# Around the last RWKV norm: output products dealt out, residual rows unscaled and loaded sooner, four up blocks among the last transposes

## What is computed

```python
rw_out, new_wkv = rwkv7_group(p_shift, ...)        # ends in: yn = (y - mu) * rsqrt(var + GN_EPS) per head
out = (yn * gn_g + gn_b + bonus) * g               # the end of rwkv7_group
mix = jnp.concatenate([rw_out, att_out], axis=-1) @ w_out
x = layer_norm(DEEPNORM_ALPHA * x + mix, ln1_g, ln1_b)
up = x @ ffn_w_up
u_conv, u_lin = up[..., :D_FF], up[..., D_FF:]     # D_FF = 2816
h = jax.nn.silu(conv(u_conv)) * u_lin
x = layer_norm(DEEPNORM_ALPHA * x + h @ ffn_w_down, ln2_g, ln2_b)
```

## Time and profile before

| | us |
|---|---|
| median of 3 runs | 1758.98 (1752.64 to 1760.13) |
| profiled execution | 1760.66 |
| its span, first to last instruction | 1758.6 |
| TensorE busy | 1618.3 (92%) |
| VectorE busy | 921.3 (52%) |
| ScalarE busy | 684.9 (39%) |
| GpSimd busy | 336.0 (19%) |
| mean granted clock of TensorE | 0.947 of 2.4 GHz |

### The profile page before, as it was taken

One profiled execution on the slowest core, in us unless ns is written; L12 is line 12 of the kernel. 1 busy time (PEld: TensorE's weight loads), 2 busy tenths in 40 slices (PEclk: granted clock), 3 DMA queues, 4 the chain that ended last, 5 costly groups with the idle time before them and its releaser, 6 DMA issues.

```text
span 1758.6 us, 39976 instructions
## 1 busy us (share of the span) xinstructions
PE 1618.3 (92%) x17211; PEld 1167.1 (66%) x17211; DVE 921.3 (52%) x2144; ACT 684.9 (39%) x1162; POOL 336.0 (19%) x209
## 2 busy tenths in 40 slices
PE   6989999998999778988767979999999999999998
PEld 4457666664667566666646856666666666888887
DVE  3579999985768557767431762333322222100046
ACT  5633233114677546665533233333333333411110
POOL 2431111002211101221112011111111222121100
PEclk9789999998999789988878989999999999999999
DMA  5232122235622112100114221111111111421002
GB/s 217 72 116 98 49 70 78 76 103 169 184 54 59 29 45 80 40 22 3 51 35 150 85 88 49 48 48 49 49 48 49 48 48 49 176 73 49 25 16 85
DMA packets 50113, 126.69 MB, mean 72 GB/s; under 512 B 17266, under 2 KB 24082, under 8 KB 42098
## 3 DMA queue, kind: packets, MB, share of 16 engines
q1 hardware_dynamic: 48850, 123.08, 20.7%
q0 software_dynamic: 1088, 1.05, 0.2%
HBM read 100.34 MB, written 23.77 MB: 71 GB/s over the span
## 4 chain that ended last, share of the span: by engine, by line
PE 82%; DVE 7%; ACT 5%; issue 3%; DMA 1%; SPq 1%; DVEq 0%; ACTq 0%
PE bank L2272 79%; PE bank L2429 1%; PE bank L1013 1%; PE bank L958 1%; DVE arena L2022 1%; DMA arena<-x 1%; DVE arena L2065 1%; ACT L1394 1%; ACT arena L2476 0%; DVE arena L2035 0%; SPq L765 0%; DVE arena L1636 0%; DVE arena L2018 0%; SPq L769 0%; DVE arena L2019 0%
## 5 line engine op out<-in xcount | busy, mean ns | idle before, releaser
L2272 PE MATMUL bank<-arena 64*64 64x64 f32 (+10 forms) x16504 | 1533.6, 289 | 121.8 <-issue 22.1
L2272 PEld LDWEIGHTS bank<-arena 128*128 128x128 f16 (+6 forms) x16504 | 1089.8, 124 | 564.2 <-issue 140.0
L2783 POOL TENSOR_TENSOR arena<-arena 128x2048 f16<-128x2048 f32 x53 | 215.8, 4073 | 826.5 <-ACT arena L2476 826.5
L2671 DVE TENSOR_SCALAR_CACHE_REDUCE arena<-arena 128x384 bf16<-128x384 f32 (+6 forms) x231 | 196.9, 918 | 1.2
L2475 ACT ACTIVATE arena<-arena 128x2048 f16<-128x2048 f32 x53 | 100.8, 1902 | 158.0 <-PE bank L2272 139.3
L2076 DVE TENSOR_SCALAR arena<-arena 128x1072 f32<-128x1072 f32 x22 | 18.9, 859 | 186.7 <-issue 173.8
L2492 ACT ACTIVATE arena<-bank 128x352 f32<-128x352 f32 x72 | 33.4, 464 | 192.6 <-PE bank L2272 192.6
L1770 POOL TENSOR_TENSOR arena<-arena 128x512 f32<-128x512 f32 x40 | 54.4, 1368 | 259.5 <-PE bank L2272 127.0
L2476 ACT ACTIVATE arena<-arena 128x2048 f32<-128x2048 f32 x53 | 100.6, 1898 | 0.0
L2088 DVE SCALAR_TENSOR_TENSOR arena<-bank,arena 128x352 f32<-128x352 f32 (+1 forms) x66 | 33.9, 514 | 120.4 <-PE bank L2272 93.5
L2003 ACT ACTIVATE arena<-arena 128x1056 f16<-128x1056 f32 x22 | 23.9, 1085 | 131.0 <-DVE arena L2090 131.0
(11 more groups left out here) (269 smaller groups left out, 1176.1 us busy)
## 6 DMA issues: line engine op xcount, KB each, us to landing
arena<-slabs SPq DMA_DIRECT2D x53, 1024.0 KB, 4.9
arena<-kcache SPq DMA_DIRECT2D x32, 256.0 KB, 2.9
arena<-vcache SPq DMA_DIRECT2D x32, 256.0 KB, 3.0
prw<-arena SPq DMA_DIRECT2D x42, 176.0 KB, 1.9
arena<-xt SPq DMA_DIRECT2D x4, 1056.0 KB, 10.2
x1d<-arena SPq DMA_DIRECT2D x8, 512.0 KB, 2.6
arena<-x1d SPq DMA_DIRECT2D x1, 4096.0 KB, 13.0
y<-arena SPq DMA_DIRECT2D x8, 512.0 KB, 2.6
```

Of the source, the lines that this page charges most:

```text
L2272: return nc.tensor.matmul(out, lhsT, rhs, start=start, stop=stop, skip_group_check=True)
L2671: last = dve.tensor_scalar(junk, a, s, None, op, ALU.add, accum_out=cnt[:, k:k + 1])
L2783: pool.tensor_tensor(WL[r].rearrange("p a b -> p (a b)"), STG[s], WH[r].rearrange("p a b -> p (a b)"), ALU.subtract).then_inc(slab_lo, 1)
```

## The change

- `out` is dealt: token tile 0 after `ch` 7, tile 1 after `cen`, tile 2 after `var`, tiles 3 and 4 after `zg` of the last period. All five now belong to item 7.
- The last item's `YS, SQ, YC, RSTD, FO` move to another place in `arena` (`NORM`), which frees the place of residual rows 5 to 8 once `y` of item 7 is read. SP waits for that, loads these rows ahead of slab 17, then slab 17, the norm's parameters and slab 18. Its wait for the last `wkv_p` stores stands before slab 19.
- No residual row is scaled by ALPHA, here and before the second norm: products are added with UN / ALPHA, and LN_EPS is divided by ALPHA squared. `resid_scaled` is gone. VectorE waits for the first five rows before the first residual, for the others after the first sampled part.
- GpSimd's split of slab 16 waits until `y` of item 7 is read.
- Four up blocks (f = 0 and 1, m = 0; n = 0 and 1) are made inside `ln1_order`: n = 0 after "t1" 6, n = 1 after "t1" 7. Their ScalarE copies stand at the same places.

```diff
 RW_PERIOD = (
...
+    ("fin", "a", 1), ("ch", "c", 2), ("bo", "a"), ("lp", "b", 4), ("zg", "d"), ("out", "d", 3), ("out", "d", 4), ("fin", "a", 2), ("fo", "d", 2), ("scale", "p", 0), ("ch", "c", 3),
...
+    ("zgate", "z0"), ("bv", "a"), ("y", "c"), ("split", "s", 0), ("ch", "c", 7), ("out", "c", 0), ("lp", "a", 1), ("ss", "p"), ("zscan", "z0"), ("cen", "c"), ("out", "c", 1),
+    ("gh", "b"), ("scan", "p"), ("lx", "a", 1), ("zsquare", "z0"), ("var", "c"), ("out", "c", 2), ("km", "p"), ("zkm", "z0"), ("ry", "b"), ("lp", "a", 2),
...
-            if not 0 <= items[who] < NI or (kind == "out" and k < NI + 2) or (kind == "fin" and k == 1):
+            if not 0 <= items[who] < NI or (kind == "out" and items[who] != NI - 1) or (kind == "fin" and k == 1):
...
         if t >= 2:
             steps.append(("t1", t - 2))
+        if t == TQ:
+            steps += [("up", (0, 0)), ("up", (1, 0))]
+        if t == TQ + 1:
+            steps += [("up", (0, 1)), ("up", (1, 1))]
     return steps
...
+        NORM = [(YS, SQ, YC, RSTD, FO)] * (NI - 1) + [tuple(words(XT0 + HT * n, HT) for n in range(5))]
...
-            def out(i):
-                out_halves(SL_OUT, range(4, KT), range(OUT_EARLY))
+            def out(_, t):
+                out_halves(SL_OUT, range(4, KT), (t,))
...
-            def ch(i, n):
-
-                if i == NI - 2 and n < X1E:
-                    if n == 0:
-                        act.wait_ge(resid_in, 16)
-                    act.activation(X1[:, n, :], X1[:, n, :], ACT.Copy, scale=ALPHA)
-
...
             def wsplit(n):
+                if n == 1:
+                    emptied(pool, ("y", NI - 1))
                 split(SL_OUT + n)
...
         def late_sync(sp, load_slab):
-            sp.wait_ge(mx_ready, 1)
+            emptied(sp, ("y", NI - 1))
+            sp.dma_start(X1[:, X1E:TQ, :], i["x"][P * X1E:T].rearrange("(t p) n -> p t n", p=P)).then_inc(resid_in, 16)
+            sp.dma_start(X1[0:NS, TQ, :], i["x"][T:TOK]).then_inc(resid_in, 16)
             load_slab(SL_OUT + 2)
+            sp.dma_start(LN1P.rearrange("p a b -> p (a b)"), i["ln1"].broadcast_to([P, 2 * DM])).then_inc(ln1_in, 16)
             load_slab(SL_OUT + 3)
-            for t in range(X1E, TQ):
-                sp.dma_start(X1[:, t, :], i["x"][P * t:P * t + P]).then_inc(resid_in, 16)
-            sp.dma_start(X1[0:NS, TQ, :], i["x"][T:TOK]).then_inc(resid_in, 16)
-            sp.dma_start(LN1P.rearrange("p a b -> p (a b)"), i["ln1"].broadcast_to([P, 2 * DM])).then_inc(ln1_in, 16)
+            sp.wait_ge(wkv_out, 16 * HP)
...
+                if kind == "up":
+                    emptied(pe, ("t1", (2, 5)[t[1]], 1))
+                    cols(SL_UP + t[0], (0,), (t[1],))
+                    continue
...
         def late_scalar(act, link, split):
 
-            act.wait_ge(resid_in, 16 * (1 + TQ - X1E + 1))
-            split(SL_OUT + 2)
-            act.activation(X1[:, X1E:TQ, :], X1[:, X1E:TQ, :], ACT.Copy, scale=ALPHA)
-            act.activation(X1[0:NS, TQ, :], X1[0:NS, TQ, :], ACT.Copy, scale=ALPHA).then_inc(resid_scaled, 1)
-            for w in (SL_OUT + 3, SL_UP, SL_UP + 1):
+            for w in (SL_OUT + 2, SL_OUT + 3, SL_UP, SL_UP + 1):
                 split(w)
...
-            act.wait_ge(resid_in, 16 * (TQ - X1E + 4))
-            act.activation(Y2, Y2, ACT.Copy, scale=ALPHA)
-            act.activation(Y2S[0:NS], Y2S[0:NS], ACT.Copy, scale=ALPHA).then_inc(resid_scaled, 1)
...
         def late_vector(dve, link):
-            dve.wait_ge(resid_scaled, 1)
-            dve.wait_ge(ln1_in, 16)
+            dve.wait_ge(resid_in, 16)
...
                 part(n)
+                dve.wait_ge(resid_in, 16 * 3)
                 for t in (first, TQ, *range(first + 1, TQ)):
                     residual(n, t)
+            dve.wait_ge(ln1_in, 16)
```

More of the change, by code:

```diff
@@ L337, in late_banks @@
             continue
+        if kind == "up":
+            b.add(("col", SL_UP + t[0], 0, t[1]), "act")
+            continue
         for w in (SL_OUT + 2, SL_OUT + 3):
@@ L341, in late_banks @@
     for f in range(FT):
-        cols(SL_UP + f, by=("act", "dve"))
+        if f < UP_EARLY:
+            b.add(("col", SL_UP + f, 0, 2), "act")
+            cols(SL_UP + f, (1,), by=("act", "dve"))
+        else:
+            cols(SL_UP + f, by=("act", "dve"))
     for n in range(4):
@@ L1109, in cen @@
                 emptied(pe, ("y", i))
-                channel_sums("cen", i, CEN, YS)
+                channel_sums("cen", i, CEN, NORM[i][0])
             def var(i):
                 emptied(pe, ("cen", i))
-                channel_sums("var", i, ONES2, SQ)
+                channel_sums("var", i, ONES2, NORM[i][1])
             def zg(i):
                 low_rank(i, "zg")
-            def out(i):
-                out_halves(SL_OUT, range(4, KT), range(OUT_EARLY))
+            def out(_, t):
+                out_halves(SL_OUT, range(4, KT), (t,))
             rows_of = lambda h4: slice(NS * h4, NS * h4 + NS)
@@ L1399, in fo @@
                 emptied(act, ("zg", i))
-                act.activation(MXH[0][:, i // 2, HT * (i % 2):HT * (i % 2) + HT], FO, ACT.Copy, scale=XS).then_inc(fo_hi, 1)
+                act.activation(MXH[0][:, i // 2, HT * (i % 2):HT * (i % 2) + HT], NORM[i][4], ACT.Copy, scale=XS).then_inc(fo_hi, 1)
             def zgate(_):
@@ L1476, in rw_scalar @@
             steps = {"lmix": lmix, "ltanh": ltanh, "scale": scale, "gate": gate, "square": square, "scan": scan, "ln": ln, "norm": norm, "tl": tl, "am": am, "bv": bv,
-                     "lp": level_products, "wz": wz, "ry": ry, "ch": ch, "cen": cen, "var": var, "rstd": rstd, "fo": fo,
+                     "lp": level_products, "wz": wz, "ry": ry, "cen": cen, "var": var, "rstd": rstd, "fo": fo,
                      "zgate": zgate, "zscan": zscan, "zln": zln, "znorm": znorm, "split": wsplit, "ztl": ztl, "za2": za2, "zwt": zwt,
@@ L1898, in late_tensor @@
             for f in range(FT):
-                cols(SL_UP + f)
+                if f < UP_EARLY:
+                    cols(SL_UP + f, (0,), (2,))
+                    cols(SL_UP + f, (1,))
+                else:
+                    cols(SL_UP + f)
             last_g = len(DN_G) - 1
@@ L1986, in late_scalar @@
                 u = UPB[:, f % 2, :]
-                for n in range(3):
+                for n in range(2 if f < UP_EARLY else 0, 3):
                     b = wait_job(act, ("col", w, 0, n))
@@ L2294, in three, with cols @@
                 return last
-            def cols(w, ms=(0, 1)):
+            def cols(w, ms=(0, 1), ns=range(3)):
                 pe.wait_ge(slab_lo, w + 1)
@@ L2300, in cols @@
                 for m in ms:
-                    for n in range(3):
+                    for n in ns:
                         b = open_bank(pe, ("col", w, m, n))
```

35 lines of the change are left out of this document (22 added, 13 removed), and 3 rows, old and new, of the table RW_PERIOD.

## The result

| | before | changed |
|---|---|---|
| median, us | 1758.05 (1752.64 to 1760.13, 4 runs) | 1716.61 (1713.03 to 1721.34, 4 runs) |
| ratio | | 0.9768 (0.9749 to 0.9787) |
| span of the profiled execution | 1758.6 | 1713.0 |
| mean granted clock | 0.947 | 0.963 |

The kernel is 41.4 us faster by the medians; 33.8 were forecast, with a range that ended 1.4 us above what came. The question is where 8 us more came from (12 by the two profiled spans).

What follows compares the result with a forecast made beforehand. TensorE's own work was taken as 82% of the path, so gains must come where it idles or is slow. Terms 1.6 + 3.4 + 5.3 + 10.1 + 4.3 + 9.1 = 33.8 us gave 1725.2 us, range 1718 to 1739.

Steps and rivals of the forecast that it cites:

- Part 1: Between products of RWKV items 6 and 7: ScalarE no longer scales five residual rows; gain 1.6 us, bounds 0 to 2.85.
- Sum 1.6 us: Same place: TensorE's waits behind the scaling ACTIVATEs, some 1.0 us and 0.6 us, taken as the whole gain.
- Part 2: Item 7's state steps: moving GpSimd's slab 16 split shortens item 6's mxl; gain 3.4 us, bounds 0 to 3.4.
- Part 3: Last item's norm: five output tiles dealt over it, y's end to mx_ready 18.4 to 13.1; gain 5.3 us, bounds 2.7 to 7.4.
- Parts 4 and 5: Output stage: unscaled, earlier-loaded residual rows remove TensorE's hole, 10.1 us; low clock after two pauses goes, 4.3 us.
- rival C: Output stage: a new wait for a slab or rows, 5 us and half the clock; about 1732 us; chance 0.09.
- Part 6: Last transposes before up projection: four up blocks fill TensorE's holes, 7.6 us, plus clock 1.5; gain 9.1, bounds 5 to 9.4.
- the 1.7 us gap stays: After the last transpose: TensorE's 1.73 us wait for the last evacuation was to remain despite the up blocks.
- A: Last item's norm: clock stays low, 2.7 us gained instead of 5.3, output stage begins at 0.50; 1730.5 us; chance 0.17.
- B: RWKV items 6 and 7: parts 1 and 2 hidden by another wait; 5.0 us less, 1730.2 us; chance 0.10.
- D: Last transposes: the up blocks fill nothing; 9.1 us less gain, 1734.3 us; chance 0.06.
- E: Up or down projection: lower clock for d us costs d/2; chance 0.04 for d over 85, 0.04 for 50 to 85.

Runs made afterwards that it cites:

- u_split: Changed kernel without GpSimd's wait for y of item 7 ahead of slab 16's split; y 6 to y 7 took 22.1 us, no whole time given.
- u_deal: Changed kernel with all five output tiles again between ch 7 and cen of the last item; 1728.26 us, ratio 0.9831 to the kernel before.
- again_after: Changed kernel, unchanged, profiled once more; 875.3 us from y of item 5 to the end.
- u_rescale: Changed kernel with only ScalarE's scaling of residual rows back; mx_ready to the first transpose 54.2 us, no whole time given.
- u_load: Changed kernel with only the late row loads back, after mx_ready and two slabs; mx_ready to the first transpose 54.2 us, no whole time given.
- The longer row: Changed kernel, unchanged, timed again with five rounds; median 1720.35 us, ratio 0.9767 to the kernel before.

## Why the prediction was right or wrong

**Part 1** was mis-sized most for its size: 1.6 forecast, 3.4 came in the first pair (31.7 - 28.3), and 3.8 between the means of the four executions with the ACTIVATEs (31.4) and the eleven without (27.6). Its direct half was right, 0.63 + 1.03 us of waits; the step that failed is "Sum 1.6 us", and with it the high bound of 2.85, which left out the lower clock of the 68 products behind the waits (4.66 us for 3.01).

**Part 2**: 3.4 forecast, 3.45 came in the first pair (22.13 - 18.68), and u_split gives the cause. That is the upper end: with the split in its new place the stage has two lengths, 18.7 and 19.6, and the means of nine such executions and of the four with the old place are 2.7 apart.

**Part 3**: 5.3 forecast; 18.4 to 11.6 is 6.8, but at the same rise of the clock it is 5.2 (u_deal). The forecast's chain put the rise 3.9 us after y's end, as before. It came after 0.6. In again_after it came after 3.9, and there `cen` was read at 4.35 for the 4.3 of the forecast, Ln ended at 7.4 for 7.4, and mx came at 13.2 for 13.1. So the working was right, and the 1.5 more is luck; the means of the four executions with the tiles in one piece and the nine with them dealt out, 17.4 and 12.2, give 5.2 too.

**Parts 4 and 5**: 10.1 + 4.3 = 14.4 forecast, 68.7 - 54.2 = 14.6 came. The clock was 1.00 in the whole stage. What the text missed is that either half of the edit does it alone: it gave the gain to the loads and to the scaling together, and rival C (a new wait of 5 us) reckoned a late slab or row at a price, though VectorE's adds can start 7 us after mx, or stop for 5.5, at no cost, as u_rescale and u_load show.

**Part 6**: 9.1 forecast, 10.8 came (771.7 - 760.9), 11.5 and 12.1 by other pairs. The filled holes are the 7.6 of the forecast. The step that failed is "the 1.7 us gap stays": it shrank to 0.77. VectorE's evacuations for the last transposes, before and changed:

```profile
1030.66 2.86 DVE L2065 SCALAR_TENSOR_TENSOR arena<-bank,arena 128x512 f16<-128x512 f32 x6
```

```profile
1003.25 0.54 DVE L2083 SCALAR_TENSOR_TENSOR arena<-bank,arena 128x128 f16<-128x128 f32 x2 [4.91 <-ACT arena L1995]
```

Before, four evacuations of the tiles ahead stood in front of the last two; now they were over 4.9 us before these. The rest is mostly the clock. At the start of the up projection it is worth 1.6 to 2.9 us by execution (725.0 to 726.3 from there to the end, against 709.1 + 14.3 for the four early blocks, the 14.3 being an estimate from 96 products at 0.149), where 1.5 was forecast. The last transposes, 1.06 us before and 0.68 now, are 0.4 more that no term had. Some 0.3 us stay unexplained.

**The sum.** From y 5 on the first pair of profiles differs by 39.1 us for 33.8 forecast: 1.8 more in part 1, 1.5 in part 3 (the phase of the clock), 0.2 in parts 4 and 5, 1.7 in part 6. Over all such profiles it is 38.3. By the means of all executions of either form, which leave less to luck, the terms are 3.8 (part 1), 2.7 (2), 5.2 (3), 15.0 (4 and 5) and 11.4 (6), some 38 in all, where 1.6, 3.4, 5.3, 14.4 and 9.1 were forecast: so parts 1 and 6 are the terms that were mis-sized, by 2.2 and 2.3 us. The profiled spans held 6.5 us more, and the first medians 3, which must come from the stretch without any edit, as far as marks and medians can be set side by side. The fault in the range was its lower end, 1718. The terms' high bounds gave 37.5 us of gain, 1721.5, and only 3.5 us were put under that for executions of one kernel that differ, though those of before already lay 7.5 us apart; and two high bounds were themselves passed, that of part 1 (2.85) by 0.6 to 0.9 us and that of part 6 (9.4) by 1.4 to 2.7. The longer row's median, 1720.35, lies inside the range.

**Rivals.** A (low clock through the norm) describes four of the nine executions with part 3 in the changed kernel's form, but costs 1.5 us and not 5.3, since the clock was up before mx_ready each time. B, C and D are out: parts 1 and 2 show in y 5 to y 7, no new wait stops TensorE, and the holes are filled. E (lower clock in the long stages) is out: the stage from the transpose on is 760.8 to 760.9 in every kernel with part 6. Of the marks that were named, the last transposes were to end near 1014; they end at 1003.1, of which 6.5 us are the early stretch, 3.3 parts 1 and 3, and the rest small differences behind mx.

## What to carry to other kernels

Price a wait of TensorE twice: the time it stands still, and the half clock of the products behind it, if rows show it there (the pause of 1.77 us ahead of mx cost none). Here the second came to half of part 1, 1.8 of the 14.5 us of parts 4 and 5, and a sixth to a quarter of part 6. When a stall has two causes of which either can be hidden by the banks, undo them one at a time before giving both credit. And cut executions at marks: a stage without an edit tells how much of a difference is luck. Where a stage has two lengths from one execution to the next, as three have here, size a part from several executions of either form, not from the first pair of profiles.

## What was not expected of the hardware

TensorE's granted clock differs between executions of the same program at the same place: 82 products at about 396 us took 7.92 us in 2 executions and 12.7 to 12.9 in the other 13, and after the add for y of item 7 the clock rose 0.6 to 3.9 us late in executions of one order of products. The stages tell what this can be worth: the one ahead of y 5 varies by 6.8 us, the next three by 1.5, 0.9 and 1.6, the last two, with TensorE busy nearly throughout, by 0.1. That is enough for the single times of the changed kernel, 1713 to 1723 us, though only the profiled ones can be cut. And a VectorE instruction with two SBUF inputs took 0.69 us alone; begun 0.5 us into a GpSimd split it took 4.13 (two executions), begun 1.4 us into it 3.22 (two more), and each time it ended 0.5 us after the split.
